# Two latent attentions begin with keys prepared earlier and queries in two pieces; the first group's norm comes from running statistics

## The reference, cut to what matters

```python
def mixing_sublayer(h, hc, w_in, rpb, w_s, b_s, g_sgu, g_q, g_k, g_out, w_o, need_ctx_out):
    qa, ka, va, zb, qc, kc, vc = split_cols(h @ w_in, IN_SIZES_2)          # also for the context
    kc_x = rms_norm(heads(kc_x, GQA_KV_HEADS), g_k)
    o_a = neighbourhood_attention(...)                                      # 6 heads, bias rpb
    o_b = spatial_gating(jax.nn.gelu(zb), w_s, b_s, g_sgu)
    q_c = apply_axial_rope(rms_norm(heads(qc, GQA_Q_HEADS), g_q), cos, sin)
    k_c = apply_axial_rope(rms_norm(heads(kc, GQA_KV_HEADS), g_k), cos, sin)
    o_c = gqa_latent(q_c, k_c, heads(vc, GQA_KV_HEADS), kc_x, vc_x)         # 6 heads on 2 key heads
    y = merge_groups(o_a, o_b, o_c, g_out) @ w_o

def merge_groups(o_a, o_b, o_c, g_out):
    return jnp.concatenate([rms_norm(o_a.reshape(B, N, D_A), g_out[:D_A]),
        rms_norm(o_b, g_out[D_A:D_A + D_B]),
        rms_norm(o_c.reshape(B, N, D_C), g_out[D_A + D_B:])], axis=-1)      # 384, 256, 384 columns

def rms_norm(x, g):
    return (x * lax.rsqrt(jnp.mean(x * x, -1, keepdims=True) + LN_EPS)) * g
```

## Time and profile before

| | |
|---|---|
| median of 3 runs | 3411.35 us (3409.27 to 3413.03) |
| the profiled execution's own time | 3412.68 us |
| its span | 3410.9 us |
| mean granted clock of TensorE | 0.993 |
| busy: PE, PEld, DVE, ACT, POOL | 97%, 90%, 49%, 39%, 14% |
| TensorE's waits for `OL` (L3076) | 8.0 us in 4 |
| attention of layer 0 | from about 1745 us to 1901 us |
| attention of layer 1 | from about 2785 us to 2911 us |

### The profile page before, as it was taken

The page is one execution under the profiler, slowest core; times in us unless marked ns, Lnnn a source line. Parts: engine busy times, 40 slices in busy tenths (PEclk is TensorE's granted clock), DMA queues, the critical chain, the costliest instruction groups (busy, mean ns, idle before and its releaser), DMA issues. The chain is left out here.

```text
span 3410.9 us, 60342 instructions
## 1 busy us (share of the span) xinstructions
PE 3300.4 (97%) x24858; PEld 3073.3 (90%) x24874; DVE 1682.7 (49%) x2815; ACT 1338.3 (39%) x2368; POOL 478.2 (14%) x471
## 2 busy tenths in 40 slices
PE   8999999999899999999999999999999999999998
PEld 7999987887688999998789889999998789889998
DVE  4666543556624456765545672222227545643334
ACT  4222322347623332235448563122125547542224
POOL 1010010146300111011013101001010114010100
PEclk9999999999999999999999999999999999999999
DMA  4444422222133344542101421111223212313232
GB/s 167 161 170 171 133 80 69 62 72 59 34 99 94 101 146 173 180 158 99 57 17 48 127 85 57 62 61 63 63 73 120 90 39 71 124 63 93 88 96 90
DMA packets 94975, 325.24 MB, mean 95 GB/s; under 512 B 10801, under 2 KB 15153, under 8 KB 94577
## 3 DMA queue, kind: packets, MB, share of 16 engines
q1 hardware_dynamic: 90992, 307.19, 28.0%
q0 software_dynamic: 3280, 13.68, 1.2%
q10 hardware_dynamic: 432, 0.52, 0.0%
HBM read 309.96 MB, written 2.10 MB: 91 GB/s over the span
## 5 line engine op out<-in xcount | busy, mean ns | idle before, releaser
L2356 DVE TENSOR_TENSOR r_Wbasel<-r_Wf,r_Wbaseh 128x1024 fp32r<-128x1024 f32 (+1 forms) x298 | 376.5, 1264 | 564.4 <-ACT r_Wbaseh L1739 564.1
L1739 ACT ACTIVATE r_Wbaseh<-r_Wf 128x1024 fp32r<-128x1024 f32 (+1 forms) x298 | 307.9, 1037 | 449.4 <-PE PS L1132 352.7
L1130 PE MATMUL PS<-r_X1h,r_Wbaseh 128*128 128x264 f32 (+2 forms) x1216 | 391.5, 322 | 13.4 <-DVE r_X1l L2593 3.5
L1130 PE MATMUL PS<-r_X2h,r_Wbaseh 128*128 128x256 f32 (+1 forms) x1224 | 373.9, 305 | 7.5 <-POOL r_X2l L3153 3.7
L1131 PE MATMUL PS<-r_X1l,r_Wbaseh 128*128 128x264 f32 (+2 forms) x1216 | 378.2, 311 | 0.0
L1132 PE MATMUL PS<-r_X1h,r_Wbasel 128*128 128x264 f32 (+2 forms) x1216 | 377.7, 311 | 0.0
L1132 PE MATMUL PS<-r_X2h,r_Wbasel 128*128 128x256 f32 (+1 forms) x1224 | 366.6, 299 | 0.0
L1131 PE MATMUL PS<-r_X2l,r_Wbaseh 128*128 128x256 f32 (+1 forms) x1224 | 364.3, 298 | 0.0
L2356 DVE TENSOR_TENSOR r_Wtopl<-r_Wf,r_Wtoph 128x1024 fp32r<-128x1024 f32 (+1 forms) x165 | 198.9, 1205 | 280.3 <-ACT r_Wtoph L1739 280.1
L1130 PEld LDWEIGHTS PS<-r_X1h,r_Wbaseh 128*128 128x128 f32 x1216 | 229.9, 189 | 37.8 <-issue 9.0
L1130 PE MATMUL PS<-r_X2h,r_Wtoph 128*128 128x256 f32 x872 | 248.2, 285 | 3.5 <-POOL r_X2l L3153 3.5
(11 more groups left out here) (422 smaller groups left out, 9138.0 us busy)
## 6 DMA issues: line engine op xcount, KB each, us to landing
r_Wf<-in_wmod SPq DMA_DIRECT2D x96, 512.0 KB, 3.6
r_Wf<-in_f_in SPq DMA_DIRECT2D x88, 512.0 KB, 4.4
r_Wf<-in_g_in SPq DMA_DIRECT2D x88, 512.0 KB, 3.5
r_Wf<-in_g_out SPq DMA_DIRECT2D x56, 448.0 KB, 3.4
r_Wf<-in_w_o SPq DMA_DIRECT2D x40, 512.0 KB, 3.6
r_Wf<-in_f_out SPq DMA_DIRECT2D x32, 448.0 KB, 4.2
r_Wf<-in_f_out SPq DMA_DIRECT2D x16, 512.0 KB, 4.4
r_Wf<-in_w_v SPq DMA_DIRECT2D x16, 512.0 KB, 3.5
```

The lines of the kernel that those rows point to most:

```text
L1130: self.e.matmul(o, wh, xh, start=first, stop=False)
L1739: e.activation(p.w(i, cols)[0], p.Wf[:, i % NW, 0:cols], ACT.Copy).then_inc(*p.hi.did(i))
L2356: e.tensor_tensor(l, p.Wf[:, i % NW, 0:cols], h.bitcast(F32), ALU.subtract).then_inc(*p.lo.did(i))
```

## The change

It has four parts.

1. **Keys of head 6.** The two `KSA` copies (ACT) and the low half on DVE move from behind the fence to projection step s = 14, behind its weight splits and ahead of the GELUs of `ZU`; the low half on POOL moves to the end of POOL's projections, ahead of its barrier mark. For this `KSA`, `KLA`, `VC` and `SQ3` change places in memory.
2. **Queries of head 6** are made in two pieces, 128 columns and the rest, on ACT and DVE. The first unit waits for the first piece alone.
3. **Group 0's norm.** The ACT squares are gone. While head 5 runs, DVE takes `bn_stats` and `bn_aggr` of each tile of `OT` right behind that tile's output; at the end mean squared plus variance plus eps gives what the sum of squares gave. The attention's barrier mark on DVE is set behind the last output and ahead of its statistics. Feature blocks 3 and 4 go first, then the root (`groups`), then blocks 5 to 7, then the scaling of the tiles (`scales`, context tiles first in layer 0), then as before. `("ahead", 3)` moves behind the eight feature blocks.
4. **Fillers**: 9, 14, 8 and 9 become 2 each.

```diff
@@ -274,12 +274,14 @@
...
         self.RTA, p = at("RTA", [128, 1, 512], F32, p)
-        self.VT, _ = at("VT", [128, 4, 768], F32, p)
+        pv = p
+        self.VT, pe = at("VT", [128, 4, 768], F32, p)
         self.PTA, p = at("PTA", [128, 2, 768], F32, P7)
-        self.SQ3, p = at("SQ3", [128, 384], F32, p)
-        self.KSA, p = at("KSA", [128, 2, 768], F32R, p)
+        self.VC, p = at("VC", [128, 6, 128], F32, p)
+        assert p <= pv
+        self.SQ3, _ = at("SQ3", [128, 384], F32, pe)
+        self.KSA, p = at("KSA", [128, 2, 768], F32R, pv)
         self.KLA, p = at("KLA", [128, 2, 768], F32R, p)
-        self.VC, p = at("VC", [128, 6, 128], F32, p)
         self.BR, p = at("BR", [128, 2, 768], F32, P5)
@@ -623,9 +625,9 @@
...
 FILL = {("fa", "f1", 0, 0): 7, ("yb", 6): 4, ("mean", "a0", 1): 11, ("mu", "a0", 2): 13, ("hm", 0, 0, 0): 2,
-        ("hm", 0, 0, 1): 4, ("a", "l0", 0): 9, ("oo", 0, 0, 0): 14, ("bvar", "d0"): 16, ("fa", "g0", 0, 1, 4): 5,
+        ("hm", 0, 0, 1): 4, ("a", "l0", 0): 2, ("oo", 0, 0, 0): 2, ("bvar", "d0"): 16, ("fa", "g0", 0, 1, 4): 5,
         ("fa", "g0", 0, 2): 17, ("fa", "g0", 0, 2, 4): 3, ("var", "d0", 1): 5, ("mean", "d0", 2): 13,
-        ("qk3", 1, 2, 2): 20, ("qk3", 1, 2, 2, 4): 3, ("hm", 1, 0, 0): 2, ("a", "l1", 0): 8, ("oo", 1, 0, 0): 9,
+        ("qk3", 1, 2, 2): 20, ("qk3", 1, 2, 2, 4): 3, ("hm", 1, 0, 0): 2, ("a", "l1", 0): 2, ("oo", 1, 0, 0): 2,
         ("mu", "b1", 1): 6, ("square", "b1", 1): 3, ("var", "b1", 1): 8, ("fa", "g1", 0, 1): 21,
@@ -821,8 +823,9 @@
...
     order = [3, 4, 5, 6, 7, 0, 1, 2]
-    items = [("open", "top", p.fence(f"att{l}")), ("ahead", 3)] + [("of", l, ci, k) for k in order[:5]]
-    items += [("early", l, m, 0) for m in (0, 1)] + [("of", l, ci, k) for k in order[5:]]
+    items = [("open", "top", p.fence(f"att{l}"))] + [("of", l, ci, k) for k in (3, 4)] + [("groups", l)]
+    items += [("of", l, ci, k) for k in (5, 6, 7)] + [("scales", l)]
+    items += [("early", l, m, 0) for m in (0, 1)] + [("of", l, ci, k) for k in order[5:]] + [("ahead", 3)]
     for m in range(8):
@@ -982,7 +985,8 @@
...
                     bias = p.BR[:, h % 2, b:b + 256]
-                head.append(Unit(m, h, i, half, blocks, ready, out, (), bias, keys))
+                begin = [(p.dve, ("sq_begin", l)), *ready[1:]] if h == 6 and i == 0 else ready
+                head.append(Unit(m, h, i, half, blocks, begin, out, (), bias, keys))
                 if h in (5, 11):
@@ -1821,6 +1825,8 @@
...
             self.end_tile("w2_o", (l, m), True)
+        elif what == "groups":
+            self.group_root(a[0], 0, 6)
         elif what == "of":
@@ -2185,6 +2191,11 @@
...
             self.tick(l, s)
+            if s == 14:
+                e.wait_ge(*p.dve.of(("hs", l, 2, 1)))
+                e.wait_ge(*p.dve.of(("turned", "x", l, 2)))
+                self.latent_keys(l, 6)
+                self.latent_second_keys(l, 6)
             if s < 10:
@@ -2248,6 +2259,10 @@
...
         q = (p.QA if h < 6 else p.QC)[r0:r0 + 64, h % 6 // 2, 0:nq]
+        if h == 6:
+            e.activation(p.QSA[0:64, 0, 0:128], q[:, 0:128], ACT.Copy).then_inc(*p.act.did(("sq_begin", l)))
+            e.activation(p.QSA[0:64, 0, 128:nq], q[:, 128:nq], ACT.Copy).then_inc(*p.act.did(("sq_high", l, h)))
+            return
         e.activation(p.QSA[r0:r0 + 64, h % 2, 0:nq], q, ACT.Copy).then_inc(*p.act.did(("sq_high", l, h)))
@@ -2302,18 +2317,12 @@
...
         self.latent_queries(l, 6)
-        self.latent_keys(l, 6)
-        self.latent_second_keys(l, 6)
         self.attention(p.latent_units[l])
...
     def output(self, l):
-        p, e = self.p, self.e
-        nz = 6 - 2 * l
         self.fence(f"att{l}")
-        for i in range(nz):
-            self.group_squares(l, i, 0)
-        self.group_root(l, 0, 6)
+
     def output_high(self, l, ci, f):
@@ -2406,6 +2415,10 @@
...
             self.moments(*a)
+        elif what == "groups":
+            self.group_root(a[0], 0, 6)
+        elif what == "scales":
+            self.group_scale(a[0], (4, 5, 0, 1, 2, 3) if a[0] == 0 else range(4))
         elif what == "apply":
@@ -2891,6 +2904,21 @@
...
                         p.SM[:, 8 + 2 * (u % 4):9 + 2 * (u % 4)], None, ALU.mult).then_inc(*p.dve.did(("o", A.id, u)))
+        if u == len(A.units) - 1:
+            self.bar(f"att{A.l}")
+        if d.h == 5:
+            self.group_stats(A.l, d.i, u)
+
+    def group_stats(self, l, i, u):
+
+        p, e = self.p, self.e
+        st = p.SM[:, 16 + 6 * (i % 2):22 + 6 * (i % 2)]
+        e.wait_ge(*p.dve.of(("o", f"l{l}", u)))
+        if i >= 2:
+            e.wait_ge(*p.dve.of(("gag", l, i - 2)))
+        e.bn_stats(st, p.OT[:, i, 0:384]).then_inc(*p.dve.did(("gst", l, i)))
+        e.wait_ge(*p.dve.of(("gst", l, i)))
+        e.bn_aggr(p.SM[:, 90 + 2 * i:92 + 2 * i], st).then_inc(*p.dve.did(("gag", l, i)))
@@ -2949,6 +2977,8 @@
...
             self.tick(l, s)
+            if s == 14:
+                self.latent_low_keys(l, 6)
             if 11 <= s < 15:
@@ -2991,9 +3021,11 @@
...
         nq = 768 - 256 * l
-        e.wait_ge(*p.act.of(("sq_high", l, h)))
-        e.tensor_tensor(p.QSA[64:128, 0, 0:nq], p.QC[0:64, 0, 0:nq], p.QSA[0:64, 0, 0:nq].bitcast(F32),
-                        ALU.subtract).then_inc(*p.dve.did(("sq_low", l, h)))
+        for a, z, high, low in ((0, 128, ("sq_begin", l), ("sq_begin", l)),
+                                (128, nq, ("sq_high", l, h), ("sq_low", l, h))):
+            e.wait_ge(*p.act.of(high))
+            e.tensor_tensor(p.QSA[64:128, 0, a:z], p.QC[0:64, 0, a:z], p.QSA[0:64, 0, a:z].bitcast(F32),
+                            ALU.subtract).then_inc(*p.dve.did(low))
@@ -3039,7 +3071,7 @@
...
         nz = 6 - 2 * l
-        for g in range(a // 6, z // 6):
+        for g in range(max(a // 6, 1), z // 6):
             x = p.SM[:, 32 + 6 * g:32 + 6 * g + nz]
@@ -3052,16 +3084,22 @@
...
         self.latent_low_queries(l, 6)
-        self.latent_low_keys(l, 6)
         self.attention(p.latent_units[l])
-        self.bar(f"att{l}")
...
         nz = 6 - 2 * l
-        self.group_root(l, 0, 6)
-        for i in range(nz):
+        x, y = p.SM[:, 32:32 + nz], p.SM[:, 90:102].rearrange("p (i c) -> p i c", c=2)
+        e.wait_ge(*p.dve.of(("gag", l, nz - 1)))
+        e.tensor_tensor(x, y[:, 0:nz, 0], y[:, 0:nz, 0], ALU.mult).then_inc(*p.dve.did(("gmean", l)))
+        e.wait_ge(*p.dve.of(("gmean", l)))
+        e.scalar_tensor_tensor(x, x, 1e-6, y[:, 0:nz, 1], ALU.add, ALU.add).then_inc(*p.dve.did(("groot", l, 0)))
+
+    def group_scale(self, l, tiles):
+        p, e = self.p, self.e
+        for i in tiles:
             o = p.OT[:, i, 0:384]
+            e.wait_ge(*p.dve.of(("grecip", l, 0)))
             e.tensor_scalar(o, o, p.SM[:, 72 + i:73 + i], None, ALU.mult).then_inc(*p.dve.did(("scaled", l, i, 0)))
```

## The result

The changed kernel takes 3387.55 us (median of 4 runs, 3385.38 to 3392.99) against 3411.41 (4 runs); the ratio is 0.9933, 95% interval 0.9916 to 0.995. Run once more beside later experiments it took 3390.56 against 3412.27, ratio 0.9941 (0.9929 to 0.9954). It is faster by well over 0.2%, near the forecast of 3392 and inside the range. The profiled execution has a span of 3387.7 us (own time 3389.52), 23.2 less than before.

A forecast was written before the change was run, and what follows sets the result against it. TensorE, busy 97%, was taken as the bound, so only its waits and fillers count. Gains 6.3 - 1.7 + 9.0 + 7.6 = 21.2 us, less 1.2 for the clock, gave 3391.4, rounded 3392; range 3386 to 3402.

The forecast's parts named there:

- The starts: At both attention starts the first exponential comes earlier, 3.1 us at layer 0 and 3.2 at layer 1, together 6.3.
- The price of the pieces: At layer 0's attention start the 128-column query piece takes 0.31 us on ACT, its low half 0.3 to 0.4 on DVE.
- The moved keys: Two ACT key copies ahead of the `ZU` GELUs delay TensorE: 1.7 us lost at layer 0, nothing at layer 1.
- The clock there: Half clock after TensorE's pause of some 2.6 us at layer 0's s = 14: 0.7 counted, one fall costing up to 1.7.
- The clock elsewhere: Half clock in layer 1's sparse first output tile: 0.5 us counted as lost.
- rival with falls at all thin places: Clock falls at both starts, s = 14 and both first tiles: 8.5 us lost instead of 1.2, hence 3399; chance 0.12.
- Layer 0's end: From layer 0's last attention output to TensorE's restart 9.85 us gained, less 0.8 for late weight splits: net 9.0.
- zero for the earlier statistics: Statistics of the five earlier tiles, 0.75 us each on DVE during head 5, cost nothing; bounds 0 and 0.8.
- The residual at tile 3: Layer 0's output stage: late weight splits on DVE delay residuals, TensorE loses 0.8 us; bounds 0 and 2.3.
- Layer 1's end: Restart behind layer 1's last attention output at 2920.9 against 2928.48: 7.6 us gained, with no cost from the splits.
- slower rival: Late weight splits starve the output projections of both layers: 41 us lost, 3433; chance 0.03.
- Half the ends: DVE, with weights, residuals and context features, bounds the output stage: some 9 us of the ends' gain lost, 3401; chance 0.12.

The follow-up runs named there:

- combined: Changed kernel with head 6's keys ahead of s = 14's weight copy, first unit's gate statistics behind its maximum, one late weight split (two at layer 1) earlier: 3386.45 us.
- Keys first: Changed kernel with head 6's key copies and DVE key low ahead of the weight copy of s = 14 instead of behind it: 3386.86 us, ratio 0.9926 to before.
- swapped order: Changed kernel with ACT's two key copies at s = 14 in the other order: 3391.74 us, one run.
- starts only: Changed kernel with part 3 undone and the old 14 and 9 fillers back at the first output tiles: 3405.11 us, ratio 0.9987 to before.
- splits in front: Changed kernel with `("ahead", 3)`, three output-projection weight splits, back at the head of the output sequence: 3395.23 us, ratio 0.9952 to before.
- squares back: Changed kernel with ACT's squares at the head of its output list and no batch statistics on DVE: 3396.32 us, ratio 0.9961 to before.
- filled pause: Changed kernel with eight more fillers ahead of the last value turn of s = 14 in layer 0: 3388.01 us, ratio 0.9939 to before.

## Why the prediction was right

- **The starts: 6.3 forecast, 6.63 measured** (3.30 and 3.33). The price of the pieces held: 0.31 for ACT's first as estimated, 0.28 on DVE (0.3 to 0.4). That the exponential is paced by DVE and not by the scores' start was right at layer 0 (combined gained 0.44 by taking the statistics away). At layer 1 scores and DVE nearly tie, 0.1 apart, and taking the statistics away gained 0.04: the reason given does not hold there. It cost the sum nothing.
- **The moved keys: 1.7 forecast, 1.6 measured**, the wait at 2.43 for the 2.5 expected, and none at layer 1. Keys first shows that nothing else of it was on the path.
- **The clock there: 0.7 forecast, 1.5 in the first trace.** This term was mis-sized: 0.7 of at most 1.7 is a fall in two cases of five, and it came right behind the pause in seven of nine traces. In the other two a fall of 1.1 came at the attention's start instead.
- **The clock elsewhere: 0.5 counted at layer 1's first tile, none measured.** The two errors offset each other. The working did not see that the kernel before had a fall at that very tile, so that one went there instead of coming. The rival with falls at all thin places is out: neither the changed kernel nor the one without any fillers shows one at a new output tile or at layer 1's start. At layer 0's start two of the traces with the pause at s = 14 show one (1746 and 1750) and the three without it none, too few to tell the start from the pause.
- **Layer 0's end: 9.0 forecast, 8.29 measured.** From the first feature turn to the restart before took 17.71 and now 8.66, 9.05 gained for 9.85. Most of the 0.8 between them is the zero for the earlier statistics: they delay the last output by 0.64, within the bounds of 0 and 0.8. The residual at tile 3 cost 0.76 for the 0.8 forecast, and combined gives just that back. The statistics of 384 columns took the 0.56 of the estimate.
- **Layer 1's end: 7.6 forecast, 7.39 measured**, restart 9.70 behind the last output for 9.5.
- **The sum:** 20.0 forecast, 18.6 by the stretches of the first pair (1720.66 on), 19.7 by those of the second trace after. The medians moved by 23.9 and 21.7. In the first pair of traces the part beyond lies in the stretch with unchanged instructions; of the medians' other runs no trace shows where it lies. So the changed stretches gained a little less than forecast and the medians more, and the total's closeness owes something to luck. Two slips in the working matter little: 3391.4 is written as 3392, and the clock rival's 8.5 instead of 1.2 takes 7.3 off the gain, leaving 12.7 and not 14 (its 3399 follows from the 12.7).
- **The slower rival** is out: no wait for a weight's low half appears in the output stages, and DVE's splits catch up within three tiles. **Half the ends** is out with `o0` and `o1`.

## What to carry to other kernels

When work moves from a serial place to an earlier one, look at what the engine has directly behind the new place: two copies in front of the GELUs that free banks cost 1.6 us and brought a half-clock stretch of 1.5 to 1.7, and cost nothing one weight copy earlier. Statistics that an engine can take as each tile is finished beat a pass over all tiles behind the last one, though they push the last tile back by nearly their own length (0.64 for a pair of 0.75). Fillers set for an old wait must be reset with it: here half of the gain would have gone into them.

## What the runs showed of the hardware

**DVE and POOL in each other's way.** A subtraction of 64x768 with two operands in SBUF takes POOL 1.80 to 1.82 alone and DVE 0.94 to 0.95 when it is first. With both at once the later one pays most: POOL 2.58 to 2.63 when both begin together (1.8 and DVE's 0.8), DVE 2.44 when POOL began 0.47 earlier, ending 0.81 behind POOL's end at 1723.48. That is mainly one waiting for the other. POOL, when first, took 2.10, which is 0.3 more than alone; what this 0.3 is stays open. The Trainium skill (SBUF — State Buffer, "SBUF: two separate sides") has it as an exclusive lock on the shared port pair, held for the whole instruction by whichever starts first. By that rule the swapped order, with DVE 0.04 ahead, had to give DVE back its 0.95, and the trace agrees. In the kernel before, POOL's record begins 0.02 ahead (1747.48 and 1747.50) and DVE still took 0.94: starts that close do not tell in a trace which was first. Here DVE's 1.5 lay in idle time and cost nothing.

**The clock behind a pause.** In the kernels without the pause at s = 14, the 1.5 at each attention start was followed by no half clock. Of the nine pauses of 2.4 to 2.6 at s = 14 seven had a half-clock stretch begin within 0.6 of their end; in the other two traces it came 23 us later, at the attention's start. Those of 3.05, 3.61 and 3.69 at layer 0's first output tile had one within 2.5 of their end, and so had at layer 1's first output tile those of 2.95 (before, starts only), 1.88 (splits in front) and 1.59 (squares back). But the 2.8 of the kernel without fillers was not (it came 20 us behind the half clock of s = 14), nor was a pause of 1.61 at its first output tile. So the pause's length alone does not tell it; what else does stays open. The Trainium skill (TensorE: Matmul & The Clock Gate, "What's actually happening") says that the throttled clock is the default and activity releases it; the filled pause agrees, since with the same arrival of `ZU` (3.97 behind the weight copy's start, 3.98 in the changed kernel) its one trace has no fall. Where a fall lands varies from trace to trace of one kernel, 1724 and 1750 here. The unchanged 1720 us vary by up to 5.6, and falls are only part of it: squares back has 24 us of half clock there like the kernel before and is 5.6 shorter.
